# A two-layer hybrid decoder trunk: table products eight side by side and at the layer's beginning, both parts of x in one product, banks awaited one by one

## What is computed

```python
h = rmsnorm(x, norm_mix[l])
u, sq, sk, sv, dq, dk, dv, gate_logits = split(h @ w_in[l])        # 7 x 512, 3 x 1024 columns
y_ssm = gelu(s5_ssm(u, ...)); a, b = split(y_ssm @ ssm_w_glu[l]); y_ssm = a * sigmoid(b)
y_sb = stick_breaking_attention(sq, sk, sv)                         # 8 heads x 64
o = differential_attention(rope(dq), rope(dk), dv, lam)             # 4 heads, p1 - lam * p2
y_da = rmsnorm(o, diff_subln[l]) * (1.0 - lam_init)
proj = einsum('bsnc,ncd->bsnd', stack([y_ssm, y_sb, y_da]), w_branch[l])
x = x + sum(sigmoid(gate_logits) * proj, axis=2) @ w_out[l]
xq = rmsnorm(x, norm_cross[l]) @ w_xq[l]; xk, xv = split(rmsnorm(mem, norm_mem[l]) @ w_xkv[l])
x = x + softmax(xq @ xk.T / sqrt(128)) @ xv @ w_xo[l]               # 4 heads
x = x + square(relu(rmsnorm(x, norm_mlp[l]) @ w_up[l])) @ w_down[l] # hidden 4096
```

## Time and profile before

| | |
|---|---|
| median of 3 runs | 1072.11 us (1070.06 to 1073.37) |
| the profiled execution | 1070.78 us |
| its span | 1069.1 us |
| mean granted TensorE clock | 0.990 |
| PE busy | 1020.3 us (95%), 8056 instructions |
| DVE busy | 741.8 us (69%) |
| ACT busy | 559.0 us (52%) |
| DMA, mean over the span | 165 GB/s |

### The profile page before, as it was taken

The page is one execution under the profiler, slowest core; times in us unless marked ns, Lnnn a source line. Parts: engine busy times, 40 slices in busy tenths (PEclk is TensorE's granted clock), DMA queues, the critical chain, the costliest instruction groups (busy, mean ns, idle before and its releaser), DMA issues. The chain is left out here.

```text
span 1069.1 us, 20083 instructions
## 1 busy us (share of the span) xinstructions
PE 1020.3 (95%) x8056; PEld 926.4 (87%) x8056; DVE 741.8 (69%) x1112; ACT 559.0 (52%) x831; POOL 47.0 (4%) x100
## 2 busy tenths in 40 slices
PE   6989999999998999999989999999999989999996
PEld 6868799899897899988879779998998869999995
DVE  5957897868865756886455459877887557555554
ACT  7346525457565646445453564364657556444442
POOL 5001200000000004000000030000000000000000
PEclk9999999999999999999999999999999999999998
DMA  8524436535543555543445543363554435555551
GB/s 327 178 80 146 138 114 213 196 130 184 185 153 114 190 180 195 181 175 138 164 153 175 189 150 122 117 197 139 170 185 160 155 119 178 186 189 189 185 191 66
DMA packets 58284, 176.28 MB, mean 165 GB/s; under 512 B 14416, under 2 KB 16464, under 8 KB 58064
## 3 DMA queue, kind: packets, MB, share of 16 engines
q1 hardware_dynamic: 58048, 174.99, 47.6%
...
q10 hardware_dynamic: 144, 0.00, 0.0%
HBM read 171.82 MB, written 3.15 MB: 164 GB/s over the span
## 5 line engine op out<-in xcount | busy, mean ns | idle before, releaser
L1216 DVE TENSOR_TENSOR s_w_lo<-s_raw,s_w_hi 128x1024 fp32r<-128x1024 f32 x312 | 374.2, 1228 | 131.6 <-ACT s_w_hi L843 127.3
L843 ACT ACTIVATE s_w_hi<-s_raw 128x1024 fp32r<-128x1024 f32 x312 | 321.3, 1054 | 209.6 <-PE p_T L1764 135.3
L1762 PE MATMUL p_T<-s_hT_hi,s_w_hi 128*128 128x256 f32 x1088 | 311.8, 287 | 0.1
L1763 PE MATMUL p_T<-s_hT_lo,s_w_hi 128*128 128x256 f32 x1088 | 308.4, 283 | 0.0
L1764 PE MATMUL p_T<-s_hT_hi,s_w_lo 128*128 128x256 f32 x1088 | 308.4, 283 | 0.0
L1762 PEld LDWEIGHTS p_T<-s_hT_hi,s_w_hi 128*128 128x128 f32 x1088 | 209.2, 192 | 4.8 <-issue 3.2
L1763 PEld LDWEIGHTS p_T<-s_hT_lo,s_w_hi 128*128 128x128 f32 x1088 | 209.4, 192 | 0.5
L1764 PEld LDWEIGHTS p_T<-s_hT_hi,s_w_lo 128*128 128x128 f32 x1088 | 209.3, 192 | 0.0
L1762 PE MATMUL p_A<-s_w_hi,s_bT_hi 128*128 128x512 f32 x320 | 125.2, 391 | 2.4 <-DVE s_bT_lo L1216 2.4
L1763 PE MATMUL p_A<-s_w_lo,s_bT_hi 128*128 128x512 f32 x320 | 124.7, 390 | 0.0
L1764 PE MATMUL p_A<-s_w_hi,s_bT_lo 128*128 128x512 f32 x320 | 124.6, 389 | 0.0
...
## 6 DMA issues: line engine op xcount, KB each, us to landing
...
```

Of the source, the lines that this page charges most:

```text
L843: return nc.scalar.activation(o, i, f, **kw)
L1216: return V.tensor_tensor(o, i0, i1, op)
L1762: mm(o, lhi, rhi, start=first, stop=False, **kw)
L1763: mm(o, lhi, rlo, start=False, stop=False, **kw)
```

## The change

- **Up units.** `hT_hi` and `hT_lo` become one tile `hT` with the two parts side by side. For each k and ft there is one product of 512 columns (w_hi times both parts) and one of 256 (w_lo times the hi part), 32 instead of 48 a unit. Each ft has a bank of its own: T0, T1 for up(g, 0) and X0, X1 for up(g, 1). ACT copies the second half of each bank, DVE adds the first half to it and does Relu and square in one instruction.
- **p_k.** Its products are the stage `mm_k` now, in two banks, eight tiles of 64x32 side by side and not four; there are still 160. The diagonal's product has 64 rows. ACT's copies are 16 of 32 rows and half as many columns, instead of 8.
- **Layer 1's table products.** `mm_k` and `mm_bt(1, 0)` stand at the beginning of layer 1 between the two turn_x of mix; the other three `mm_bt` after units 3, 4, 5. Before, p_k and p_bt stood after down and up units of layer 0. The table stages of DVE and ACT for layer 1 move by some units.
- **Layer 0.** lam_sum, lam_exp, lam go from units 3, 4, 5 to 12, 13, 14 (their data lie in mem_t, not uB: the DMA queue waits for lam before it loads mem_t, and no more before it loads uB). p_params goes to 15, a p_bv to 7, p_bt to 9 and 10. The stages of unit 6 are sorted by RANK too.
- **da_n(0) and gelu_split** go to unit 24, from 22 (layer 1's gelu_split from 21). DVE does its later part of da_s between the two chunks of the next unit, not behind both.
- **Banks.** A unit's banks are awaited one by one, each just before its first product. In N units that close their banks a signal `half_rows` is given when the first 128 rows are done, and their evacuation starts then. turn_x does the transposes of rows 0 to 127 in both banks first.

```diff
         after(-1, "turn_x", "mix", 0)
+        after(-1, "mm_k", 1)
+        after(-1, "mm_bt", 1, 0)
         after(-1, "turn_x", "mix", 1)
...
-        after(3, "lam_sum")
-        after(4, "lam_exp")
-        after(5, "lam")
-        after(13, "p_params", 0)
+        after(12, "lam_sum")
+        after(13, "lam_exp")
+        after(14, "lam")
+        after(15, "p_params", 0)
...
-        pre(0, dict(ct=-1, cv=(3, 4), b0=5, bv=(6, 8), k=(6, 7), bt=(8, 8, 10, 10), ph=(9, 10, 11)))
+        pre(0, dict(ct=-1, cv=(3, 4), b0=5, bv=(7, 8), ph=(9, 10, 11)))
+        blocks((6, 6, 7), ((9, 9), (9, 9), (10, 10), (10, 10)))
...
+        blocks((None, 0, 1), ((None, 0), (3, 3), (4, 4), (5, 5)))
...
-    after(first + 9, "gelu_split")
+    after(24, "gelu_split")
...
-    after(22, "da_n", 0)
+    after(24, "da_n", 0)
...
-        return ["T0", "T1"][key[2]:][:1]
+        return ["T0", "T1"] if key[2] == 0 else ["X0", "X1"]
...
-        [[["A0", "A1"], ["X0", "X1"]][s[1]][s[2] % 2]] if s[0] == "p_bt" else
-        [["A3", "X0"][s[1]]] if s[0] == "p_k" and s[2] == 0 else
+        [["A1", "A0"][s[2] % 2]] if s[0] == "mm_bt" else
+        [["A3", "A2"], ["T0", "T1"]][s[1]] if s[0] == "mm_k" else
...
-        hT_hi, hT_lo = sb("hT_hi", [P, KD, T], F32R), sb("hT_lo", [P, KD, T], F32R)
+        hT = sb("hT", [P, KD, 2, T], F32R)
+        hT_hi, hT_lo = hT[:, :, 0, :], hT[:, :, 1, :]
...
+        def rows_done(u, t):
+
+            return (chunk_done, 2 * u + 2) if t else (half_rows, by_rows.index(u) + 1)
...
-                    sp.wait_ge(*st.at(lam_made, 1))
...
+                        sp.wait_ge(*st.at(lam_made, 1))
...
+                    t, h = s[1:]
+                    use = ("mm_k", t)
+                    b, o = stage_banks(use)[h], PC * h
+                    act.wait_ge(*st.at(*full_at(l, b, use)))
+                    every = kt[:, :, :].rearrange("p (m q) c -> p q m c", q=4)
+                    for q in range(4):
+                        src = bank[b][32 * q:32 * q + 32, 0:4 * PC].rearrange("p (m c) -> p m c", c=PC)
+                        fn(every[o:o + 32, q, :, :], src).then_inc(*st.mid())
+                        ins = fn(every[o + 32:o + 64, q, :, 32:PC], src[:, :, 0:32])
+                        ins.then_inc(*st.sig(*freed(l, b, use))) if q == 3 else ins.then_inc(*st.mid())
...
-                        take(r_b[i], b[0], key, ACT.Relu)
+                        act.wait_ge(*st.at(chunk_done, 2 * u + 2))
+                        for j, bk in enumerate(b):
+                            ins = fn(r_b[i][:, j * T:j * T + T], bank[bk][:, T:2 * T])
+                            ins.then_inc(*st.sig(up_copied)) if j else ins.then_inc(*st.mid())
...
-                    dve.wait_ge(*st.at(chunk_done, 2 * AT_UNIT[key] + 2))
                     for t, b in enumerate(banks):
+                        dve.wait_ge(*st.at(*rows_done(AT_UNIT[key], t)))
...
-                        dve.wait_ge(*st.at(*freed(l, b[0], key)))
-                        tt(q_b[i], r_b[i], r_b[i]).then_inc(*st.sig(sq_made))
+                        dve.wait_ge(*st.at(up_copied, 2 * g + i + 1))
+                        for j, bk in enumerate(b):
+                            tt(r_b[i][:, j * T:j * T + T], r_b[i][:, j * T:j * T + T], bank[bk][:, 0:T], ALU.add)\
+                                .then_inc(*st.sig(*freed(l, bk, key)))
+                        dve.wait_ge(*st.mine())
+                        V.scalar_tensor_tensor(out=q_b[i], in0=r_b[i], scalar=0.0, in1=r_b[i], op0=ALU.max, op1=ALU.mult)\
+                         .then_inc(*st.sig(sq_made))
...
+                    scores = [s for s in SIDES[l][u] if s[0] == "da_s"]
                     for n in nxt[n_first:]:
-                        prep(n)
+                        prep_chunk(2 * n)
+                        for s in scores:
+                            dve.wait_ge(*st.mine())
+                            later(s)
+                        prep_chunk(2 * n + 1)
                     for s in SIDES[l][u]:
-                        dve.wait_ge(*st.mine())
-                        later(s)
+                        if s not in scores:
+                            dve.wait_ge(*st.mine())
+                            later(s)
...
-                    if opens(key):
-                        for b in banks:
-                            pe.wait_ge(*st.at(*before(l, b, ("down",) if key[0] == "down" else key)))
+                    use = ("down",) if key[0] == "down" else key
...
+                                parts = key[0] == "up"
+                                if half == 0 and k == 0 and (parts or ft % 2 == 0):
+                                    pe.wait_ge(*st.at(*before(l, banks[ft if parts else ft // 2], use)))
+                                if parts:
+                                    o = bank[banks[ft]]
+                                    mm(o[:, :], wh[:, k, c], hT[:, ks, :, :].rearrange("p r n -> p (r n)"),
+                                       start=(half == 0 and k == 0), stop=False, skip_group_check=True)
+                                    ins = mm(o[:, 0:T], wl[:, k, c], hi[:, ks, :], start=False,
+                                             stop=(half == 1 and k == kt // 2 - 1), skip_group_check=True)
+                                    continue
...
+                                if opens(key) and half == 0:
+                                    pe.wait_ge(*st.at(*before(l, banks[t], use)))
...
+                                if closes(key) and half == 1 and t == 0:
+                                    ins.then_inc(*st.sig(half_rows))
...
-                        for j, b in enumerate(stage_banks(s)):
-                            pe.wait_ge(*st.at(*before(l, b, s)))
-                            turn_rows(b, 2 * s[2] + j, x).then_inc(*st.sig(full[b]))
-                    elif kind == "p_k" and s[2] == 0:
+                            for j, b in enumerate(stage_banks(s)):
+                                if t == 0:
+                                    pe.wait_ge(*st.at(*before(l, b, s)))
+                                for k in (0, 1):
+                                    c = (4 * s[2] + 2 * j + k) * P
+                                    ins = turn(bank[b][:, k * T + t * P:k * T + t * P + P], x[:, t, c:c + P])
+                                if t:
+                                    ins.then_inc(*st.sig(full[b]))
+                    elif kind == "mm_k":
...
+                        for b in stage_banks(s):
+                            pe.wait_ge(*st.at(*before(l, b, s)))
+                        tiles = [(bank[b][32 * q:32 * q + 32, :], rows, q)
+                                 for b, rows in zip(stage_banks(s), HALVES) for q in range(4)]
+                        for m in range(STILES // 4):
                             for r in range(2):
-                                for e, rows, out_rows, p in tiles:
-                                    mm(bank[b][out_rows, PC * m:PC * m + PC], bN0[rows, r, 2 * m + e, GC:3 * GC],
-                                       ct[rows, r, 2 * m + e, :], start=(r == 0), stop=False, skip_group_check=True)
-                                for e, rows, out_rows, p in tiles:
-                                    mm(bank[b][out_rows, PC * m + GC:PC * m + PC], bN0[rows, r, 2 * m + e, 0:2 * GC],
-                                       ct[rows, r, 2 * m + e, 0:PC - GC], start=False, stop=False, skip_group_check=True)
-                            for e, rows, out_rows, p in tiles:
-                                two = slice(p, p + 2 * GC)
-                                ins = mm(bank[b][out_rows, PC * m:PC * m + 2 * GC], ident[two, two],
-                                         diag_d[two, 2 * m + e, :], start=False, stop=True, skip_group_check=True)
-                        ins.then_inc(*st.sig(full[b]))
-                    elif kind == "p_bt":
+                                for o, rows, q in tiles:
+                                    mm(o[:, PC * m:PC * m + PC], bN0[rows, r, 4 * m + q, GC:3 * GC],
+                                       ct[rows, r, 4 * m + q, :], start=(r == 0), stop=False, skip_group_check=True)
+                                for o, rows, q in tiles:
+                                    mm(o[:, PC * m + GC:PC * m + PC], bN0[rows, r, 4 * m + q, 0:2 * GC],
+                                       ct[rows, r, 4 * m + q, 0:PC - GC], start=False, stop=False, skip_group_check=True)
+                            for o, rows, q in tiles:
+                                ins = mm(o[:, PC * m:PC * m + 2 * GC], ident[rows, rows.start:rows.start + 2 * GC],
+                                         diag_d[rows, 4 * m + q, :], start=False, stop=True, skip_group_check=True)
+                                if m == STILES // 4 - 1 and q == 3:
+                                    ins.then_inc(*st.sig(full[stage_banks(s)[rows.start // PC]]))
```

(50 more changed lines are left out.)

43 lines of the change are left out of this document (21 added, 22 removed).

## The result

The changed kernel takes 1056.97 us (1055.70 to 1059.94, 4 runs), the kernel before 1071.09 (1069.41 to 1073.37, 4 runs): a ratio of 0.987, 95% interval 0.984 to 0.990. It is 14.1 us faster, and not the forecast 24.3; by the ratio that is 1058.3 on the prediction's base of 1072.1, just outside its range. The profiled execution took 1055.70, its span 1054.0, 15.1 under the one before. The sign was right, the sum was 9 us too large. Where it went is found by setting the two timelines side by side, at the first product of each unit; a term's price is the change of the difference (after less before) across its stretch.

The account below looks back on a forecast made before the run. TensorE was taken as the bound, so time comes off only by fewer or cheaper products or less waiting. The terms summed to -24.3 us: 1047.8 against the median of 1072.1, range 1037 to 1057.

Parts of the forecast that it names:

- E: Up units: 512 times, two 256-column products become one of 512, saving 13 ns each; -6.6 us.
- C: da_n and gelu_split moved to unit 24: old wait goes, da_o waits 2.0; -2.6 us layer 0, -0.8 layer 1.
- A: Start of layer 0: sv0's wait shrinks, p_k starts earlier, 1.4 of wait left at sb_u, clock holds; -6.3 us.
- B: lam stages at units 12 to 14 add VectorE work where it is the later engine; +0.3 us, bounds 0 and 1.8.
- D: xv and turn_x by halves let products start earlier: xv -1.2, turn_x -1.0; together -2.2 us.
- G: sv0 of layer 1 no longer waits for both its banks; -0.9 us.
- H: Kernel's end: residual of the first 128 rows starts six products earlier; -0.7 us.
- rival (c): Up units: VectorE comes to stand in the path that frees their banks, slower than before; 1078 us, chance 0.04.
- F: Layer boundary: layer 1's p_k fills the residual wait and the clock's fall behind it goes; -4.5 us.
- (a): Instruction refills don't bind: both p_k take some 3 us, 4.2 less each; 1039 us, chance 0.13.
- (b): New waits take back more: da_o late by 4.8, lam costs 1.8, boundary dip 2.5; 1055 us, chance 0.20.

Follow-up runs that it names:

- x13: Changed kernel with mm_k's products four side by side in the old kernel's pattern, two blocks of rows by two of columns: 1056.2 us, ratio 0.986.
- x2: Changed kernel with da_n(0) and gelu_split put back at their old units (22; layer 1's gelu_split 21): 1055.7 us, ratio 0.985.
- x3: Changed kernel with da_n(0) at unit 23 instead of 24: 1052.0 us, ratio 0.983.
- x1: Changed kernel with the up units' 512-column product split again into two of 256, all else kept: 1059.6 us, ratio 0.990.
- x9: Changed kernel with layer 1's mm_k and mm_bt(1,0) behind unit 0 instead of between the two turn_x: 1059.1 us, ratio 0.989.
- x10: Changed kernel with each of mm_k's 160 products issued twice in each layer: 1073.2 us, ratio 1.0005.

## Why the prediction was wrong, point by point

**In one sentence.** The steps that failed are E's price of a merged product (13 ns, measured 8 on the average of the 512), C's layer 1, where the old wait was taken out and the like of it not put in, and the waits inside mm_k and at da_o, left without the clock's fall behind them.

**Bounds of the kernel.** Right: TensorE's queue decides, and both sources of gain are there.

**A (-6.3, measured -4.6).** The steps held: sv0 at once, b0 at 54.8 (said 54.3), mm_k 7.9 with waits on issue inside (said 7.2), ScalarE's copies 2.7 (said 2.6). The failed step is "1.4 of wait is left and the clock holds". The clock fell earlier, inside mm_k, to 0.83 over these nine us and then 0.79, where the refill waits had grown to 1.84 and 2.38. I had counted the new waits inside the 7.2 and put nothing down for the clock: sv1 lost 1.9, which took the place of the 1.4 of wait. x13's execution with the clock at 1.00 puts the clock's part at 1.0 of the 1.7 that A fell short; mm_k's 0.7 is the rest. That the waits bring the fall is argued from the order of events: in x13 the clock held behind waits as long, so it was to be reckoned with, and not certain.

**B (+0.3, measured -0.3).** Just under its lower bound of 0: lam costs nothing at 12 to 14.

**C (-3.4, measured -0.3).** The second largest miss. For layer 0 the new wait was sized well (2.0, measured 2.29), but I let it stand without a clock price, though I had charged 1.7 of clock to the wait it replaced: glu lost 1.3, of which 0.7 are gone from the stretch in x13, where the clock held. For layer 1 I only removed the old wait and never worked the new one out; the same chain of VectorE stands there and waits the same: 2.28 at 738.88 before, 2.29 at 732.37 after, now with a fall of the clock behind it that x13 prices at 0.6. So the term came out at +1.0 and not -0.8. x2 confirms that the move is worth nothing, x3 that one unit earlier it is worth 5.

**D, G, H.** Near: -1.9 for D (said -2.2), sv0's wait of 0.83 gone, tail -0.7. Within D the wait at turn_x mostly moved to the first up unit, so that part brought 0.5 (said 1.0), and xv's 1.3 (said 1.2).

**E (-6.6, measured -3.2).** The largest miss. The term was mis-sized: I took 0.227 and 0.120 from stretches of one width each. Mixed, a pair costs 0.3528 in most units. x1 measures the merged product at 3.9 in the stretches, and a new wait of 0.7 on ScalarE at up(3, 1), which x1 shows to be another part's, takes some back. VectorE stayed clear, so rival (c) never came near.

**F and G (-5.4, measured -3.9).** Right that mm_k fills the wait on the residual (x9: 2 to 3.4 us). Wrong that no dip is left: the clock fell behind its refill waits of 2.30 and 1.65, and the 16 table products and the transposes take 3.4 (537.80 to 541.23) against 1.9 in x13 at full clock; mm_k itself took 8.0, 0.7 more than said.

**The rivals.** (a), that refills don't bind, is refuted by x10. (b), new waits that take back more, came about in part: of its three places the boundary's dip was real, da_o was late by 2.29 in each layer and not by 4.8, and lam cost nothing. That the measured time lies near its 1055 is luck, since E's 3.4, the largest part of the miss, is not in it. What neither the forecast nor (b) had is the lower clock behind layer 0's mm_k and behind both da_o: 1.0, 0.7 and 0.6 us by x13's stretches.
